# Odd mixer of a two-layer step: scan tasks in even slots, keys one level ahead, low weights in mid-chunk

## The reference

```python
def hgrn2_gates(z, lb):
    log_f = jnp.logaddexp(jnp.log(lb), jnp.log1p(-lb) + jax.nn.log_sigmoid(z))
    k = (1.0 - lb) * jax.nn.sigmoid(-z)
    return k, log_f

def gla_chunk_scan(q, k, v, log_f, s0):       # per chunk of 32 steps, S carried over
        b = jnp.cumsum(gi, axis=2)
        o_inter = jnp.einsum('bhck,bhkv->bhcv', qi * jnp.exp(b), S)
        A = jnp.einsum('bhtk,bhsk,bhtsk->bhts', qi, ki, decay)
        o_intra = jnp.einsum('bhts,bhsv->bhtv', A, vi)
        S_new = S * jnp.exp(b_last) + jnp.einsum('bhsk,bhsv->bhkv', ki * jnp.exp(b_last - b), vi)

def hgrn2_bidir(u, lb_l, s0, norm_g):
    q, zf, zb, v, g = jnp.split(u, ...)
    o_f, s_f = gla_chunk_scan(q, kf, v, gf, s0[:, 0])
    o_b, s_b = gla_chunk_scan(rev(q), rev(kb), rev(v), rev(gb), s0[:, 1])
    o = o_f + rev(o_b)
    o = rms_norm(o, norm_g) * jax.nn.silu(g)

xs = xs + gate * (hgrn2_bidir(modulated_norm(xs) @ mix1_w_in) @ mix1_w_out)
```

## Time and profile before

| | |
|---|---|
| three runs, us | 1890.68, 1894.46, 1896.68 |
| median | 1894.46 |
| the profiled execution | 1890.31 |
| its span | 1888.6 |
| busy PE / DVE / ACT / POOL | 93% / 62% / 35% / 7% |
| mean granted clock of TensorE | 0.952 |
| HBM | 138 GB/s over the span |

### The profile page before, as it was taken

One profiled execution on the slowest core, in us unless ns is written; L12 is line 12 of the kernel. 1 busy time (PEld: TensorE's weight loads), 2 busy tenths in 40 slices (PEclk: granted clock), 3 DMA queues, 4 the chain that ended last, 5 costly groups with the idle time before them and its releaser, 6 DMA issues.

```text
span 1888.6 us, 26791 instructions
## 1 busy us (share of the span) xinstructions
PE 1765.3 (93%) x9814; PEld 1634.4 (87%) x9814; DVE 1162.5 (62%) x2002; ACT 664.9 (35%) x872; POOL 135.8 (7%) x196
## 2 busy tenths in 40 slices
PE   6799999899999899999799999899898877999997
PEld 2799999677657899999799999868898877999996
DVE  2687876722322778876878886646657557853334
ACT  2334322412221543422443432243453434434322
POOL 0000000022000000000000000012110100000000
PEclk9899999999658999999899999999999988999999
DMA  9266655475102366655466655643222203644341
GB/s 323 83 181 184 184 162 166 142 232 164 39 1 68 107 184 187 186 160 166 122 184 188 184 161 167 183 140 103 81 86 75 93 28 90 189 124 132 109 127 64
DMA packets 349009, 262.05 MB, mean 139 GB/s; under 512 B 15257, under 2 KB 326802, under 8 KB 348946
## 3 DMA queue, kind: packets, MB, share of 16 engines
q1 hardware_dynamic: 325746, 191.45, 34.8%
q0 software_dynamic: 18432, 67.12, 11.2%
q10 hardware_dynamic: 4768, 2.62, 0.5%
HBM read 258.01 MB, written 3.15 MB: 138 GB/s over the span
## 4 chain that ended last, share of the span: by engine, by line
PE 86%; DVE 7%; issue 2%; SPq 2%; DMA 2%; ACT 1%; POOL 0%; ACTq 0%; DVEq 0%
PE bank L1285 24%; PE bank L1287 23%; PE bank L1286 23%; PE bank L1625 3%; PE bank L1314 2%; DVE xf L973 2%; PE bank L1583 1%; DMA ada<-in_ada_w 1%; PE bank L1303 1%; PE bank L1366 1%; DVE xl L981 1%; DVE rr L964 1%; PE bank L1561 1%; PE bank L1558 1%; PE bank L1384 1%
## 5 line engine op out<-in xcount | busy, mean ns | idle before, releaser
L852 DVE TENSOR_TENSOR w_lo<-w_raw,w_hi 128x2048 fp32r<-128x2048 f32 (+1 forms) x188 | 389.1, 2070 | 453.9 <-ACT w_hi L579 452.4
L1285 PE MATMUL bank<-xh,w_hi 128*128 128x384 f32 x1664 | 563.9, 339 | 0.3 <-issue 0.3
L1286 PE MATMUL bank<-xl,w_hi 128*128 128x384 f32 x1664 | 557.4, 335 | 0.0
L1287 PE MATMUL bank<-xh,w_lo 128*128 128x384 f32 x1664 | 557.4, 335 | 0.0
L579 ACT ACTIVATE w_hi<-w_raw 128x2048 fp32r<-128x2048 f32 (+1 forms) x188 | 325.6, 1732 | 335.7 <-PE bank L1287 301.5
L1285 PEld LDWEIGHTS bank<-xh,w_hi 128*128 128x128 f32 x1664 | 313.7, 189 | 3.4 <-issue 3.4
L1286 PEld LDWEIGHTS bank<-xl,w_hi 128*128 128x128 f32 x1664 | 313.8, 189 | 0.0
L1287 PEld LDWEIGHTS bank<-xh,w_lo 128*128 128x128 f32 x1664 | 313.3, 188 | 0.0
L875 DVE SCALAR_TENSOR_TENSOR acc<-ada,cond,acc 128x256 f32<-128x256 f32 x686 | 301.9, 482 | 10.5
L1285 PE MATMUL bank<-gg,w_hi 128*128 128x384 f32 x768 | 260.8, 340 | 1.2 <-DVE gg L1129 1.2
L1287 PE MATMUL bank<-gg,w_lo 128*128 128x384 f32 x768 | 259.6, 338 | 0.0
(11 more groups left out here) (183 smaller groups left out, 1723.7 us busy)
## 6 DMA issues: line engine op xcount, KB each, us to landing
w_raw<-in_ffn_w SPq DMA_DIRECT2D x176, 512.0 KB, 5.0
ada<-in_ada_w POOLq DMA_DIRECT2D x128, 512.0 KB, 4.0
w_raw<-in_mix_w_in SPq DMA_DIRECT2D x56, 512.0 KB, 4.6
w_raw<-in_ffn_w SPq DMA_DIRECT2D x64, 384.0 KB, 3.5
w_raw<-in_ffn_w SPq DMA_DIRECT2D x64, 320.0 KB, 3.9
first_ada<-in_ada_w SPq DMA_DIRECT2D x8, 1024.0 KB, 13.3
w_raw<-in_mix_w_out SPq DMA_DIRECT2D x16, 512.0 KB, 5.6
bias<-in_na_rpb SPq DMA_DIRECT2D x16, 96.0 KB, 6.6
```

The source lines that it names most:

```text
L852: nc.vector.tensor_tensor(w_lo[slot][:, 0:size], w_raw[slot][:, 0:size], w_hi[slot][:, 0:size].bitcast(F32), ALU.subtract).then_inc(s_lo, 1)
L1285: nc.tensor.matmul(out, ah, bh, start=first, stop=False)
L1286: nc.tensor.matmul(out, ah, bl, start=False, stop=False)
L1287: return nc.tensor.matmul(out, al, bh, start=False, stop=last)
```

## The change

The two tables of order are new, and the streams of the engines in `mix1` are rewritten around them. The number of matmuls, their shapes and the data are the same.

- **Slots.** The 40 tasks lie on an even grid, task t at eighth 30 + 10 t / 3 (rounded down): the first at eighth 6 of chunk 3, the last at eighth 0 of chunk 20. `HG_ORDER` has each pair's first three chunks earlier, and the gates g of pairs 0 to 3 as chunks 15, 17, 18 and 19.
- **Keys.** `grow_keys` of a level stands behind the answer to the level below it, and `join_keys` is issued one task ahead. POOL sums the keys first (own semaphore) and then signals its totals level by level.
- **`next_lo`** on DVE stands behind the tasks of eighths 0 to 3. On ACT the decays of a chunk stand behind the first join of the next one.
- **Reciprocals.** For pairs 0 to 2 each of the two is cut in three pieces of 128 columns, each with its product with the output, one piece behind each of the next pair's levels 0 to 5 (`root_of`). The product with the gate (`gate_y`) is separate and comes one chunk after the gate's chunk. The results stay in a tile of their own (`yn`).
- **Last pair.** `finish_last` makes head 6 and head 7 one by one, with chunk 21's `w_lo` between them. PE runs heads 0 to 5 of output chunk 0, heads 0 to 3 of output chunk 1, and then the remaining heads.

```diff
-HG_ORDER = [(0, 0), (0, 1), (0, 2), (0, 3), (1, 0), (1, 1), (1, 2), (0, 4), (1, 3), (2, 0), (2, 1), (2, 2),
...
+HG_ORDER = [(0, 0), (0, 1), (0, 2), (1, 0), (1, 1), (1, 2), (0, 3), (2, 0), (2, 1), (2, 2), (1, 3), (3, 0),
+            (3, 1), (3, 2), (2, 3), (0, 4), (3, 3), (1, 4), (2, 4), (3, 4)]
...
+    for t in range(4 * len(HG_TASKS)):
+        eighth = 8 * 3 + 6 + 10 * t // 3
+        slots.setdefault(eighth // 8, {})[eighth % 8] = (t // len(HG_TASKS), t % len(HG_TASKS))
...
+                nc.gpsimd.tensor_tensor(ksum[:, :, :], hk[b][:, 0, :, :], hk[b][:, 1, :, :], ALU.add).then_inc(s_ks, 1)
+                for lv in range(LEVELS):
+                    for d in range(2):
+                        t = block_total(pair, d, lv).rearrange("p (n two) -> p n two", two=2)
+                        ins = nc.gpsimd.tensor_tensor(block_total(pair, d, lv + 1), t[:, :, 0], t[:, :, 1], ALU.mult)
+                    ins.then_inc(s_tot, 1)
+                    pool.wait_ge(s_tot, LEVELS * pair + lv + 1)
...
+                def root_of(pair, h, c):
+                    rows = slice(c * P, (c + 1) * P)
+                    if c == 0:
+                        dve.wait_ge(s_ga, scalar_reads[fill_no[pair, "mean", h]])
+                    link(nc.vector.reciprocal(orr[h][:, rows], orr[h][:, rows]))
+                    ins = nc.vector.scalar_tensor_tensor(yn[:, 2 * pair + h, rows], ps[6 + h][:, rows], vt[:, V_HG:V_HG + 1],
+                                                         orr[h][:, rows], ALU.mult, ALU.mult)
...
+                def finish_last(h):
+                    head = 6 + h
+                    dve.wait_ge(s_ga, scalar_reads[fill_no[3, "mean", h]])
                     link(nc.vector.reciprocal(orr[h][:, :], orr[h][:, :]))
...
                     if task < LEVELS:
-                        grow_keys(pair, task)
...
                         grow_queries(pair, task)
                         for h in range(2):
                             keep_level(pair, task, h)
+                        if task + 1 < LEVELS:
+                            grow_keys(pair, task + 1)
+                        if pair and task < 2 * TB:
+                            root_of(pair - 1, task // TB, task % TB)
...
+                    slots = HG_SLOTS[i] if i in HG_SLOTS else {}
+                    for k, (pair, task) in slots.items():
+                        if k < 4:
+                            after_task(pair, task)
+                    if i == 20:
+                        finish_last(0)
+                    if 3 <= i <= 20:
+                        next_lo(n0 + i - 1)
+                    if i == 20:
+                        finish_last(1)
...
+                    for k, (pair, task) in slots.items():
+                        if k >= 4:
+                            after_task(pair, task)
+                    if i == 3:
                         ada_step(s, i)
...
+                        out_products(0, heads, 0, 4, between)
+                        pe.wait_ge(s_ol, 6)
+                        out_products(0, heads, 4, 6)
                     else:
-                        if i == 20:
-                            pe.wait_ge(s_pj, pj0[s] + 20)
-                            pe.wait_ge(s_ol, 6)
-                        pe.wait_ge(s_lo, n0 + i + 1)
-                        out_products(i, heads, 0, 6, between)
+                        pe.wait_ge(s_lo, n0 + 22)
+                        out_products(1, heads, 0, 4)
```

More of the change, by code:

```diff
@@ L742, in copy_chunk, with decays @@
                                           ).then_inc(s_st0[b], 16)
-                    next_hi(n)
+                def decays(i):
+                    pair, part = HG_ORDER[i]
+                    b = pair % 2
                     if part in (1, 2):
@@ L821, in mix1 @@
                     for k, (pair, task) in slots.items():
-                        if task in after and k == 7:
+                        if k == 7 and task in after:
                             after[task](pair)
-                    for k, (pair, task) in slots.items():
-                        if task == 9:
-                            y_hi(pair)
+                    if i < 20:
+                        next_hi(n0 + i)
                 for slot in s_sfo:
@@ L1231, in after_task, with y_lo @@
+                def y_lo(pair):
+                    for h in range(2):
+                        head = 2 * pair + h
+                        dve.wait_ge(s_oh, head + 1)
+                        nc.vector.tensor_tensor(yl[:, head, :], yn[:, head, :], yh[:, head, :].bitcast(F32),
+                                                ALU.subtract).then_inc(s_ol, 1)
                 def after_task(pair, task):
                     if task < LEVELS:
-                        grow_keys(pair, task)
                         if task == 0:
@@ L1243, in after_task @@
                             pass_state(pair, h)
-                        for h in range(2):
-                            gate_o(pair, h)
-                        if pair < 3:
-                            start_pair(pair + 1)
+                    elif task == 9 and pair < 3:
+                        start_pair(pair + 1)
+                        grow_keys(pair + 1, 0)
                 copy_rows(s, 0)
                 for i in range(22):
-                    if 0 < i <= 20:
-                        next_lo(n0 + i - 1)
@@ L1676, in run @@
                     if task == 0:
[L1677 removed]
+                        pe.wait_ge(s_ks, pair + 1)
                         for h in range(2):
```

126 lines of the change are left out of this document (71 added, 55 removed), and 6 rows, old and new, of the table HG_SLOTS.

## The result

The changed kernel takes **1862.7 us** (median of 4 runs, 1861.6 to 1863.7), the kernel before 1895.1 (4 runs, 1890.7 to 1896.7): a ratio of 0.9833, 95% interval 0.9815 to 0.985. The forecast was 1857.5, its own case 1849 to 1866. The profiled execution took 1861.57 us, with a span of 1859.9. Of the 28 executions of the kernel before that stand beside all the kernels of this document, 27 took 1889 to 1900 us and one 1856.7, at a mean granted clock of 0.968 where the six beside it had 0.943 to 0.952; no trace of it is kept, and its cause is open.

A forecast was written before the change was run, and what follows sets the result against it. PE bounds the kernel; in the odd mixer its waits, mostly for DVE, and half clock make 55.3 of 306.6 us excess. That falls to 20.6, 34.7 less: 1855.6, or 1859.8 from the median; middle 1857.5, range 1849 to 1866.

The forecast's parts named there:

- The end after chunk 19: Sign against the forecast: the part after chunk 19 takes over 46 us in place of 40.4.
- a doubled backlog: Rival: DVE's lag is twice as large, waits of 20 in place of 10 and two more bouts; 1872; chance 0.10.
- long waits that stay: Rival: PE's long waits remain because another order sets them; half of the gain, 1875; chance 0.06.
- The slower one: Rival: w_lo behind the tasks of a chunk's first half delays all 17 chunk starts; 1917 at 2.5 each; chance 0.03.
- Work: PE's matmul groups and small transposes from chunk 3 through the output projection, at full clock: 251.3 us.
- Backlog of DVE: DVE falls behind in the first six levels of pairs 1 to 3; PE waits 1.9, 2.3 and 6.0: 10.2 us.
- Start of the scan: Before chunk 4, PE waits for the last prm addition, on DVE behind level 0's answer: 2.1 us.
- The 3.1 for amat goes: At the scan's start this wait of PE vanishes, as w_lo no longer stands between the diagonal and its answer.
- POOL's ksum comes first: hidden: In the scan, POOL's key sums and totals are covered by the two tasks between; nothing if wrong by 2 us.
- End: PE's waits after chunk 19: silu 1.15, w_lo 2.1, then 0.9, first residual 1.7; 5.8 us in sum.
- Half clock: PE at 1.2 GHz behind long waits: 16.1 us before; after, one bout of 2.3 behind the wait of 2.6.
- The clock rival: Rival: many short waits lower PE's clock, each of six of 1.6 to 2.6 drawing a bout; 1869; chance 0.16.

The follow-up runs named there:

- i_pool: The change with POOL's preparation of the next pair waiting for turn of the pair before, not for level 5; 1857.4 us, ratio 0.9815.
- e_double: The change with each of the 18 reciprocal pieces of 128 columns done twice on DVE; 1878.0 us, ratio 0.9901.
- u_whole: The change with its reciprocals uncut, both heads' behind level 1 of the next pair; 1874.5 us, ratio 0.9882.
- i_ada: The change with the last ada step (small transposes and DVE's prm addition) moved into chunk 3, ahead of the first keys; 1862.7 us.

## Why the prediction was right, and where it was not

**The mechanism was right.** Long waits for DVE went; in their place stand short ones where DVE is behind, none over 3 us, with the 0.94 reciprocals, and four of the longest stand at places named (1.97 for w_lo at the start of chunk 19, 1.84 and 1.72 in the output projection, 1.11 before chunk 4). Chunk 14, also named, waited only 0.71. Not named were the 2.06 before level 0, 1.08 before a level of pair 3, and 1.07 before chunk 15, which i_pool takes away and which is thus POOL's. The end after chunk 19 took some 42 us; 40.4 was said, and 46 would have refuted it. The rivals: e_double and u_whole show what a doubled backlog and long waits that stay would have made, 1878 and 1874; 1872 and 1875 were priced for them. The slower one needed over 2.1 us at each of 17 chunk starts; there were six waits for w_lo, of 1.1 on average.

**The sizes.** Forecast for the stretch 271.9, measured 275.0. That the two are so close is in part luck, for terms of both signs were off:

- *Work*, said 251.3, is some 255.9 (256.6 by the time at 0.50). It was 4.6 or more too low, and so the 16.1 at half clock of before were too high: 11.5 if its work is the same, 13 by the time at 0.50, in 28 us of which PE was busy. The mis-sized step is the one that adds up durations of groups: it has nothing for the first main matmul behind a scan group. After a level (PE timeline, the change):

```profile
1298.85 1.50 PE L1674 MATMUL bank<-xf 128*128 128x128 f32 x12
1300.11 0.42 PE L1334 MATMUL bank<-xh,w_hi 128*128 128x384 f32 x1
1300.37 0.34 PE L1335 MATMUL bank<-xl,w_hi 128*128 128x384 f32 x1
```

  From its start to the next 0.26 us pass, where it is 0.17 between others; at some places it is 0.32 or 0.47; over the 42 such places it is 4.9. The kernel before has such places too. This time was not gained, and had been put down as gain.
- *Backlog of DVE*, said 10.2 (1.9, 2.3, 6.0 for pairs 1, 2, 3), is 7.2 (1.1, 2.6, 3.6), of which i_pool shows 2.7 to be DVE's slowing beside POOL, which no step had. Without it some 4.5, less than half of what was said. The piece of 1.25 in place of 1.33 explains 0.5 a pair; the rest of the walk's excess was not taken apart.
- *Start of the scan*, said 2.1 for prm and nothing for amat, is 1.11 and 2.06, and draws a bout of half clock that the sum did not have. "The 3.1 for amat goes" failed. Its reason, that w_lo no longer stands between the diagonal and its answer, goes against the order of the change itself, in which L869 stands ahead of L1208. And pair 0's first keys waited 1.8 us for POOL's ksum and took 2.20, then w_lo took 2.59, both stretched beside POOL (a pair of such products takes 1.1 elsewhere, a w_lo 2.28), ahead of the diagonal's keep:

```profile
1278.37 2.52 POOL L553 TENSOR_TENSOR ksum<-hk 128x768 f32<-128x768 f32 x1
...
1281.00 2.20 DVE L1192 TENSOR_TENSOR hk<-hk,hp 128x384 f32<-128x384 f32 x2 [1.81 <-POOL ksum L553]
...
1283.12 2.59 DVE L869 TENSOR_TENSOR w_lo<-w_raw,w_hi 128x2048 fp32r<-128x2048 f32 x1
```

  "POOL's ksum comes first: hidden" is the other step that fell; at pair 0 nothing hides it.
- *End*, said 5.8 (silu 1.15, w_lo 2.1, heads 0.9, residual 1.7), is 4.5 (0.96, 1.84, none, 1.72), and a bout of half clock behind the 1.84. The load of ACT's table took 1.28 and the root began at once:

```profile
1509.11 1.92 ACT L574 ACTIVATE w_hi<-w_raw 128x2048 fp32r<-128x2048 f32 x1
1511.04 1.28 ACT L800 ACT_TABLE_LOAD   x1
1512.34 1.05 ACT L800 ACTIVATE osq<-bank,lb 128x384 f32<-128x384 f32 x2
```

  The drain of about 1.38 that the Trainium skill gives in "ScalarE: Activation LUTs", section "What ACT_TABLE_LOAD costs", does not show here, as the forecast had it.
- *Half clock*, said one bout of 2.3 behind chunk 19's wait, is 3.8 (3.1 by the time at 0.50) in two, and neither is there: one is at the start of the scan, one in the output projection. The price was too high and the count too low. By the time at 0.50 before's seven bouts cost 1.9 on average and the change's two 1.6.
- *The range.* Its upper end is not the sum of its own terms: 6.8 for the backlog, 4.2 for the end and 2 for the run above 1857.5 make 1870.5, where 1866 was said. The measured time lies inside either.

Sum: +4.6 of work, -3.0 of waits (18.3 said, 15.3 measured), +1.5 of half clock = +3.1, which is 275.0 - 271.9. By the time at 0.50 it is +5.3, -3.0 and +0.8.

**The clock rival** got the smaller part of what it wanted: waits of 2.06 and 1.84 draw bouts, those of 1.97 and 1.72 don't, and in i_ada one of 1.98 does. In other kernels one of 1.66 drew a bout (i_ada, before level 0), and those of 2.04 and 2.17 in e_double drew none. So the length of the wait alone doesn't decide it here, and what does is open. The Trainium skill, "TensorE: Matmul & The Clock Gate", section "A second HAM failure mode: psum-queue depth-cycling", says that small idles between groups make the clock swing; the stretch's granted clock of 0.99, with ten waits of 0.2 to 1.1 us in it, does not bear that out. Nor does the attention stretch of the kernel before, which the forecast took for it: from 510 to 580 the clock was granted at 0.50 throughout, with PE busy all of the time, which is no swing.

**Outside the stretch** the change lost 2.9 us: 31.6 gained there, 28.7 between the profiled executions. PE's work ahead is the same, yet the first matmul of chunk 3 starts at 1273.73 (i_pool) to 1282.87 (u_whole) in the twelve profiled executions, with the kernel before at 1273.74, the earliest but one. So the 1.6 us by which the change began later are within the spread of the part before it, and the forecast, which subtracted from that early execution, took the early start along.

**What the parts are worth.** Undone one at a time, in the stretch: keys ahead 20.4 us, w_lo in mid-chunk 17.7, reciprocals cut 10.3, even slots 7.0, heads one by one 1.2 (within the spread). The first four make 55 where the whole change gives 31.6: each removes cover that the others also use, so none of these prices holds apart from the others.

## What to carry to other kernels

When one engine answers another in a loop, count its work per turn, and then place every long instruction (a conversion of weights, a reciprocal) where the longest uninterrupted stretch is shortest; cutting costs work and still wins. Ask of each step that is needed at once whether it can be asked for one turn ahead: its worth is not only its own duration but that of whatever stands ahead of it on the engine that it passes through, here up to 3.3 us of ACT's copies and w_hi and not DVE's 0.93. And when a small engine is given work beside a late one, look at the durations, not only at the waits.

## What the runs showed of the hardware

- Pairs of DVE's products with both inputs in SBUF took 2.1 to 2.6 us in place of 1.0 beside POOL's tensor operations at some places and kept their time at others, where POOL's sum took 2.5 to 2.6 in place of 1.85; reciprocals (0.94) and pairs of predicated copies from a bank (1.28) kept theirs.
- A reciprocal of 128 columns took 0.94 us, of 384 columns 2.55, of one 0.154: 6.2 ns a column; a product of two inputs took 0.55 for 384, 4.6 times less.
- Behind waits of 5.2, 3.4 and 3.5 us in u_whole PE worked at half clock (0.50 in the rows above for the first two); around 2 us the same wait at the same place was followed by half clock in one execution and by full clock in another.
- The program up to chunk 3 ended up to 9.1 us apart between the profiled executions, more than several of the effects measured here; comparing one stretch with itself took that part out.
